# Where the gate's SiLU stands in ScalarE's order, between its taps and the split of the next weights

## What is computed

```python
h = rmsnorm(x, norm2_w)
u = causal_dwconv(h @ w_up, ffn_conv_w)        # 3 taps along the tokens, 2*2816 columns
gate, up = u[..., :D_FF], u[..., D_FF:]
x = x + (jax.nn.silu(gate) * up) @ w_down
```

## Time and profile before

| | |
|---|---|
| median of 3 runs | 2517.07 us (2516.57 to 2520.61) |
| the profiled execution | 2516.36 us |
| its span on the core | 2514.6 us, so 1.8 us lie around it |
| TensorE busy | 2465.0 us, 98% of the span |
| VectorE busy | 1510.5 us, 60% |
| ScalarE busy | 1098.6 us, 44% |
| mean granted TensorE clock | 0.996 of full |

### The profile page before, as it was taken

The page is one execution under the profiler, slowest core; times in us unless marked ns, Lnnn a source line. Parts: engine busy times, 40 slices in busy tenths (PEclk is TensorE's granted clock), DMA queues, the critical chain, the costliest instruction groups (busy, mean ns, idle before and its releaser), DMA issues.

```text
span 2514.6 us, 35248 instructions
## 1 busy us (share of the span) xinstructions
PE 2465.0 (98%) x13947; PEld 2025.6 (81%) x13947; DVE 1510.5 (60%) x2483; ACT 1098.6 (44%) x1783; POOL 55.2 (2%) x110
## 2 busy tenths in 40 slices
PE   7999999999999999999999999999999999999998
PEld 5888777787788888888888788787888888888887
DVE  4234546666366766656669844565888646655555
ACT  4123247776545444446444453444333433433332
POOL 0000000000000011000000000000000000000000
PEclk9999999999999999999999999999999999999999
DMA  6322330110445565565435564423323332333332
GB/s 212 104 84 84 121 118 19 61 61 19 124 122 173 193 201 188 198 209 178 141 93 185 158 193 132 153 84 93 93 84 92 101 99 86 117 106 96 98 88 82
DMA packets 318646, 304.36 MB, mean 121 GB/s; under 512 B 10271, under 2 KB 277908, under 8 KB 318356
## 3 DMA queue, kind: packets, MB, share of 16 engines
q1 hardware_dynamic: 301956, 241.30, 32.4%
q0 software_dynamic: 14400, 56.11, 5.5%
q10 hardware_dynamic: 2128, 4.72, 0.5%
HBM read 244.41 MB, written 57.67 MB: 120 GB/s over the span
## 4 chain that ended last, share of the span: by engine, by line
PE 88%; DVE 6%; ACT 2%; issue 2%; DMA 1%; SPq 0%; DVEq 0%; ACTq 0%
PE PS L2140 15%; PE PS L2142 14%; PE PS L2141 14%; PE PS L1794 11%; PE PS L2157 7%; PE PS L2159 7%; PE PS L2158 7%; PE PS L1965 3%; PE PS L2099 1%; PE PS L1951 1%; PE PS L2075 1%; PE PS L2087 1%; DVE cg L1741 1%; DVE x L1638 1%; DMA raw<-in_w_ff 1%
## 5 line engine op out<-in xcount | busy, mean ns | idle before, releaser
L2140 PE MATMUL PS<-hh,wh 128*128 128x512 f32 x1728 | 677.8, 392 | 2.4 <-DVE hl L1611 1.6
L2142 PE MATMUL PS<-hh,wl 128*128 128x512 f32 x1728 | 673.5, 390 | 0.0
L2141 PE MATMUL PS<-hl,wh 128*128 128x512 f32 x1728 | 673.1, 390 | 0.0
L960 ACT ACTIVATE wh<-raw 128x1024 fp32r<-128x1024 f32 x352 | 366.7, 1055 | 482.5 <-PE PS L2159 343.1
L1335 DVE TENSOR_TENSOR wl<-raw,wh 128x1024 fp32r<-128x1024 f32 x286 | 346.1, 1222 | 280.1 <-ACT wh L960 279.9
L1638 DVE TENSOR_TENSOR x<-x,PS 128x512 f32<-128x512 f32 x432 | 292.6, 683 | 167.3 <-PE PS L2159 166.0
L2140 PEld LDWEIGHTS PS<-hh,wh 128*128 128x128 f32 x1728 | 325.0, 188 | 71.9 <-DVE hl L1611 3.3
L2142 PEld LDWEIGHTS PS<-hh,wl 128*128 128x128 f32 x1728 | 324.8, 188 | 68.0
L2141 PEld LDWEIGHTS PS<-hl,wh 128*128 128x128 f32 x1728 | 325.1, 188 | 66.8 <-issue 0.5
L2157 PE MATMUL PS<-fh,wh 128*128 128x512 f32 x856 | 339.1, 396 | 9.0 <-DVE x L1638 8.9
L2159 PE MATMUL PS<-fh,wl 128*128 128x512 f32 x856 | 334.2, 390 | 0.0
(11 more groups left out here) (302 smaller groups left out, 2567.6 us busy)
## 6 DMA issues: line engine op xcount, KB each, us to landing
raw<-in_w_ff SPq DMA_DIRECT2D x128, 512.0 KB, 4.0
raw<-in_w_up SPq DMA_DIRECT2D x88, 512.0 KB, 4.3
wl_s<-wl POOLq DMA_DIRECT2D x66, 512.0 KB, 5.4
wl<-wl_s SPq DMA_DIRECT2D x66, 512.0 KB, 3.5
raw<-in_w_in SPq DMA_DIRECT2D x59, 512.0 KB, 3.9
raw<-in_w_down SPq DMA_DIRECT2D x44, 512.0 KB, 5.5
raw<-in_w_out SPq DMA_DIRECT2D x32, 512.0 KB, 3.9
qkvz_s<-st POOLq DMA_DIRECT2D x16, 512.0 KB, 2.9
```

The source lines that it names most:

```text
L960: A(whs(slot), raw[:, k % 2], ACT.Copy).then_inc(s["w_hi"], 1)
L2140: mm(bank, wh[:, k % 4, cut], hh[:, kk, span(a_)], start=kk == 0, stop=False)
L2141: mm(bank, wh[:, k % 4, cut], hl[:, kk, span(a_)], start=False, stop=False)
L2142: last = mm(bank, wl[:, k % 4, cut], hh[:, kk, span(a_)], start=False, stop=kk == KT - 1)
```

## The change

The SiLU is put in the list by itself, directly behind the gate's third tap, instead of being handed to the unit "up". So it now stands ahead of ("prep", k) or ("high", k). The stages are the same, their number is the same, and all others keep their order: gate, two, silu, prep, background, up. It holds for all 44 gate tiles.

```diff
         for j in (2 * p, 2 * p + 1):
             self.single(("gate", a, j), late)
             self.put("two", a, j)
-            self.single(("up", a, j), [("silu", a, j)])
+            self.put("silu", a, j)
+            self.single(("up", a, j))
             self.put("two", a, j + FF1)
             self.act[1, a, j] = len(self.act)
             late = [("fin", a, j), ("low", 1, a, j)]
```

## The result

The changed kernel ran in 2530.32 us (median of 4 runs, 2528.84 to 2532.70) beside 2518.07 for the kernel before (4 runs, 2516.57 to 2520.61): a ratio of 1.0049, 95% interval 1.0031 to 1.0066, so slower by 8 to 17 us. Forecast were 2525.9 and a range of 2519.0 to 2529.5. The sign and the mechanism came out as forecast; the time lies 0.8 us above the range.

What follows compares the result with a forecast made beforehand. TensorE, busy 98% of the span, was taken as the bound. Four pairs 6.4 and single places 0.9, 0.4 and 1.1 made 8.8 us, 2525.2, plus 0.7 for the median: 2525.9, range 2519 to 2529.5.

Steps and rivals of the forecast that it cites:

- Nobody waits for the SiLU; the copy comes late by 2.1, the low part by 1.8: Every gate: an earlier SiLU frees nobody; the high-weight copy moves from 884.67 to 886.75, `wl` from 886.09 to 887.9.
- Most gates hide it: Pairs without background work: `wl` is done at 889.1, when the next drain has only just begun, so nothing moves.
- the rival with the uncovered loads: Loads of `raw` for later tiles land only as their copy is due: 16 us, up to 2533; chance 0.12.
- Four pairs, 1.6 each, 6.4: Half a = 0, 784 to 906 us: lag delays the first addition to x; TensorE waits 1.6 us per pair.
- The first rival: The lag is swallowed in the four pairs; only the single places stay, 0 to 2.4 us, 2517.1 to 2519.5; chance 0.16.
- ("diag"), 0.9: At 776.13, behind a `wl`: 1.8 later, done at 778.1; TensorE's ("spread") weight loads began at 777.22, costing 0.9 us.
- 1157 us, 0.4: Table load runs earlier, SiLU starts 0.6 earlier, but `rinv` moves from 1160.31 to 1160.7, costing 0.4 us.
- 1606 us, 1.1: Same exchange with a `wl` behind the copy: `hn` starts at 1611.35 against 1610.27; ends in existing TensorE waits, 1.1 us.
- The sum: Whole kernel: 6.4 + 0.9 + 0.4 + 1.1 = 8.8 us slower.
- The median of the runs lies 0.7 above that execution: Step from the profiled execution to the median: 2516.4 with 8.8 is 2525.2, with 0.7 more 2525.9.
- the forecast "about 10": TensorE's waits at the fourth group, on the addition, rise from 3 to 7 times and from 2.9 to about 10 us.

Runs made afterwards that it cites:

- the first gates alone: The kernel before, with the SiLU moved ahead of the weight split only for even j, the first gate of each pair; 2519.26 us, ratio 0.9990 to 1.0008.

## Why the prediction was right in its mechanism and missed its range

- *Nobody waits for the SiLU; the copy comes late by 2.1, the low part by 1.8.* Right: the low part stands 1.8 later, and VectorE idles 1.72 for it.
- *Most gates hide it.* Right. No copy waited for a DMA that had not before, so the rival with the uncovered loads fell.
- *Four pairs, 1.6 each, 6.4.* The waits were 1.64, 1.18, 1.64 and 1.64, 6.1 in sum, but they cost 7.3. (The pair with the 1.18 has its second drain waiting 0.62 for TensorE in the trace before, slack that I counted as none.) TensorE went on at 913.52 in a trace that is 8.22 behind at that pair, so at 905.3 as forecast. Two sizes were off. The fourth group was due earlier than the 903.7 that I counted from the drain at 899.62, for TensorE had begun with `down` at 899.42:

```profile
903.50 0.39 PE L2157 MATMUL PS<-fh,wh 128*128 128x512 f32 x1
```

  So TensorE lost 905.3 - 903.5 = 1.8. The view shows 1.64 since it counts from the end of the matmul ahead, 0.16 after the next one would have started; that it equals my 1.6 is chance. And a stop costs some 0.14 more behind it: the matmul took 0.50 and the next started 0.34 after it, against 0.39 and 0.23 in the stream; the earlier trace rows showed the 0.50 already. That is 1.94 for a pair, 0.3 more than the wait of the view.
- *The first rival*, a swallowed lag, put the threshold at 0.6 us at the first addition. By the same row it was less: the addition was done at 903.10, 0.4 ahead of the fourth group, and the kernel with the first gates alone lost 0.13 at a lag of 0.4. The lag was 2.1, so the four pairs passed either. The rival came true in the kernels that change one gate of each pair.
- *("diag"), 0.9.* The reciprocal moved 1.8, from 776.13 to 780.00 with 2.06 of it from before the part; TensorE waited 0.57 at ("spread") and lost 0.8.
- *1157 us, 0.4.* Right, with the table load as the rows gave it:

```profile
1167.70 1.28 ACT L1197 ACT_TABLE_LOAD   x1
1169.36 0.63 ACT L1197 ACTIVATE gc<-gc 128x512 f32<-128x512 f32 x1 [0.37 <-DVE gc L1650]
1169.89 1.04 ACT L961 ACTIVATE wh<-raw 128x1024 fp32r<-128x1024 f32 x1
1170.84 0.58 ACT L1242 ACTIVATE rinv<-PS 128x512 f32<-128x512 f32 x1
```

  The load ends at 1168.98, and the SiLU starts 0.38 later, when the tap is done. `rinv` is 10.53 behind 1160.31, in a kernel that was 10.17 behind when that gate's unit ended: 0.36. The Trainium skill ("ScalarE: Activation LUTs", "What ACT_TABLE_LOAD costs") adds 1.38 us of drain, which by an estimate from that figure would have held the SiLU until 1170.36; the trace has it 1.0 earlier, so the measurement decides against that rule here.
- *1606 us, 1.1.* The size is right, 1.09, the place not quite: it did not lengthen a wait that TensorE had but made a new one of 0.77 (at 1627.50; the two behind it stayed 1.08 and 1.09). So the waits on the addition are 8 and not 7; their sum, 10.1, is the forecast "about 10".
- *The sum.* 8.8 against 9.6 measured in the part, which would have been 2526.0 from the profiled execution, 2526.7 with the median: inside the range. The failed step is the level, "The median of the runs lies 0.7 above that execution". It was taken from 3 runs with a median of 2517.07, while 27 runs of the same kernel have a median of 2519.57, 3.2 above that execution, and reach from 2516.58 to 2521.82; and the range had no term for the scatter of either kernel. Of the 4.4 us between 2525.9 and 2530.32, 0.8 are the part (the stops of TensorE, mis-sized above), 2.5 the level of the kernel before, and 1.1 are left, which the scatter of four runs can hold: the changed kernel run again had a median of 2528.94, within the range. So whether the median of four runs fell just outside the range or inside it was in part luck.

## What to carry over

When an instruction that waits is moved ahead of one that is ready, cost not the instruction but the idle time that the ready one had filled, and follow it to the other engine's queue: here the low part, which waited for the copy, held back work that had nothing to do with either. Such a lag costs nothing until it passes the slack of the next hand-over and then all that lies beyond it, so two harmless moves (0.4 and about 0.4 us) can make 7.3 together. To tell a few us in 2500, compare a stretch between two fixed matmuls in both traces (it repeated to 0.04 us) and not the span.

## What was new on the hardware

- A stop of TensorE cost 0.3 us beyond the wait that the view shows: four waits of 6.1 us in sum made the stretch 7.31 longer. About 0.16 of it is how the wait is counted, from the end of the matmul ahead; the rest is a slower start behind it (0.34 to the next start, against 0.23). That slower start was there even where the addition came just in time and the trace has no idle time (904.50 with the first gates alone).
- Whether the clock fell to 1.2 GHz after a stop differed from trace to trace. After the stop of 2.03 us it did in one trace out of five and cost about 1.6 us. After a stop of 2.7 us between 1714 and 1726 us, which all ten traces have, it did in six (0.91 in 1705 to 1725 us in the kernel before, 1.00 in the changed kernel run again), and there it cost next to nothing: in all four traces with the clock at full TensorE waited another 1.1 us for VectorE instead.
- Round the idle time between two phases at 660 us the profile gives a mean clock of 0.83 in some traces and 0.74 in others, with the same program: 1.8 us less of full clock, of which the changed kernel's two traces show 1.0 us in time.
